# Expert stage of a two-block forward pass: split fp32r matmuls replaced by plain float32 on two column halves

## The chip, the cores and the metric

The kernel runs on one core of a Trainium2 chip. The metric is the device time of one execution in microseconds, the median of several runs. TensorE (PE in the profile), VectorE (DVE), ScalarE (ACT), GpSimd (POOL) and SyncE (SP) run side by side; SP issues the large transfers, and POOL issues the gathers and scatters that take their row numbers from a list.

## The reference, cut to what matters

Two blocks of layers run on 512 tokens of width 1024, all in float32. Only the last layer of the second block, a mixture of 32 experts, is touched here:

```python
expert = g_idx * EXP_PER_GROUP + e_idx           # 2 of 32 experts for each of 512 tokens
weights = g_p * e_p / jnp.sum(e_p, axis=-1, keepdims=True)
def block_mlp(args):                             # xb: the rows of one expert
    xb, e = args
    return (jax.nn.silu(xb @ w_gate[e]) * (xb @ w_up[e])) @ w_down[e]
y_pad = y_pad * w_pad[:, None]                   # each row by its token's weight
out = jax.ops.segment_sum(y_pad, tok_pad, num_segments=n_tok)
...
h = h + out                                      # then rmsnorm(h, final_norm_w) is the result
```

w_gate and w_up are 1024 x 512 and w_down is 512 x 1024 for each expert: 6 MiB an expert, 192 MiB (201.3 MB) in all.

## The kernel before

Everything but the expert layer is a chain of projections, scans and attention that fills the first 1,685 us. The weights of a product come in pieces of 1 MiB, [128, 4, 512] float32. ACT copies a piece to a rounded value (`w_hi`, type fp32r), DVE subtracts it from the raw piece (`w_lo`), and PE multiplies with both. In the trace an fp32r matmul is one matmul record, a plain float32 matmul is two, and a transpose is one.

The router gives each expert at most 64 rows (BLK = 64) with at most 15 overflow blocks after the 32 regular ones (none is needed for this input: 32 gathers run). DVE writes the token numbers of each expert's rows to `tok_of`, and POOL gathers those rows of the normalised input from `hn_dram` (`gather`, L855).

For each expert `e` the PE does, in this order (loop at the end of the tensor block):

- `gate_up(e)`: 32 fp32r matmuls of 512 columns (L1646, L1647). The stationary operand is `bT`, the 64 rows' high part beside their low part (128 columns), so one matmul gives both products; the moving operand is `e_hi` or `e_lo` (for the first two pieces `w_hi`, `w_lo`).
- `rows_T(e+1)`: 8 transposes that turn the next expert's rows (L1628).
- `down(e-1)`: 24 fp32r matmuls of 512 columns (L1667 to L1669), three for each product.
- `acts_T(e)`: 8 plain float32 matmuls with `fold`, which turn the activations and add the high and the low half (16 records at L1658; the timeline merges 8 for gate and 8 for up).

Beside that, for each expert, ACT makes six copies of a piece (L2286, L2303) and DVE six subtractions (L3164, L3280); ACT and DVE also split the rows and the activations. ACT copies the two halves of the result out (L2341), and POOL scatters them to `y_dram` by token number (L866). `y_dram` and `y_over` are zeroed earlier in the kernel (8 MiB, at 344 us). At the end SP reads `y_dram` back (`picked`, L688), DVE adds each token's two rows times their weights (`weighted`, L3330), and the last two experts' results (the `PAIR`) take another way: the last expert's `down` in plain float32 (`last_down`, L1687) and products with a matrix that puts rows to tokens (`pair_sums`, L1696), added by DVE at L3362.

Order is set by the instruction order in the source and by semaphores. SP fetches a piece of the next expert as soon as DVE has made its low part (`fetch`, L666), so one set of six raw pieces exists. In the first waits of the layer SP, POOL and the others meet at numbered stages (`together`).

## Time and profile before

| what | value |
|---|---|
| median of 3 runs | 2267.59 us (2263.74 to 2267.86) |
| profiled execution, first to last instruction (span) | 2262.9 us |
| median less span (what lies around the span, and the spread of runs) | 4.7 us |
| PE busy | 2186.2 us (97%) |
| DVE busy | 1478.4 us (65%) |
| ACT busy | 1248.5 us (55%) |
| mean granted TensorE clock | 0.987 |

The table of times holds no time of its own for the profiled execution beside its span. In the page, the busy digits are tenths in 40 slices of 56.6 us each. PE busy counts from a matmul's start to its modelled end, and matmuls overlap in the pipeline, so the pitch between starts tells the cost of one and not its duration. "128*64 128x512" means 128 contraction rows, 64 stationary columns, and a moving operand of 128 partitions x 512 columns.

### The profile page before, as it was taken

What the parts mean: (1) busy time and instruction counts of PE and PEld (TensorE: products, weight loads), DVE (VectorE), ACT (ScalarE), POOL (GpSimd) and SP (SyncE); (2) the same over time, 40 slices, a digit from 0 to 9 for tenths busy, and PEclk for the clock granted to TensorE, in tenths of its full rate; (3) what the DMA queues carried; (4) which work ended last, traced back from release to release, by engine and by line L of the source; (5) the groups of instructions that cost most, each with busy time, mean ns of one, the idle gap of its engine ahead of it and who ended that gap; (6) DMA issues with size and microseconds to landing.
All of it is one profiled execution on the core that took longest, in us unless ns stands there. A gap on an engine that the chain in (4) does not pass through costs nothing. (4 is left out here: it accounts for less than half of the span.)

```text
span 2262.9 us, 31931 instructions
## 1 busy us (share of the span) xinstructions
PE 2186.2 (97%) x12430; PEld 1731.7 (77%) x12430; DVE 1478.4 (65%) x1871; ACT 1248.5 (55%) x1696; POOL 303.7 (13%) x346
## 2 busy tenths in 40 slices
PE   7999999999999999999999999999995999999997
PEld 6878658877778787998888888888684777777774
DVE  3533862549988778765324573454447999988897
ACT  4324551468884455652315423244434889888885
POOL 2000001023320122640000000000011111122220
PEclk9999999999999999999999999999997999999999
DMA  7122117323224434011222213334146999999996
GB/s 241 57 74 93 38 38 249 124 90 93 93 84 158 148 115 150 3 59 56 90 97 93 93 43 126 112 113 149 56 155 248 399 405 412 403 404 398 401 401 255
DMA packets 121732, 385.61 MB, mean 170 GB/s; under 512 B 9549, under 2 KB 38533, under 8 KB 96401
## 3 DMA queue, kind: packets, MB, share of 16 engines
q1 hardware_dynamic: 106688, 333.54, 39.9%
q0 software_dynamic: 14416, 44.12, 5.7%
q10 hardware_dynamic: 512, 6.34, 0.7%
q8 instruction: 81, 1.33, 0.2%
q14 instruction: 35, 0.28, 0.0%
HBM read 362.89 MB, written 28.89 MB: 173 GB/s over the span
## 5 line engine op out<-in xcount | busy, mean ns | idle before, releaser
L2414 DVE TENSOR_TENSOR w_lo<-raw,w_hi 128x2048 fp32r<-128x2048 f32 x117 | 268.7, 2296 | 444.7 <-ACT w_hi L1757 444.5
L1757 ACT ACTIVATE w_hi<-raw 128x2048 fp32r<-128x2048 f32 x117 | 223.9, 1914 | 394.5 <-PE bank L918 358.2
L918 PE MATMUL bank<-hT_hi,w_hi 128*128 128x512 f32 x512 | 200.2, 391 | 2.5 <-DVE y_lo L3033 2.3
L918 PE MATMUL bank<-hT_lo,w_hi 128*128 128x512 f32 x512 | 199.5, 390 | 0.0
L918 PE MATMUL bank<-hT_hi,w_lo 128*128 128x512 f32 x512 | 199.4, 390 | 0.0
L1129 PE MATMUL bank<-hT_hi,w_hi 128*128 128x512 f32 x432 | 173.9, 402 | 0.9 <-DVE hT_lo L2478 0.9
L1129 PE MATMUL bank<-hT_hi,w_lo 128*128 128x512 f32 x432 | 168.2, 389 | 0.0
L1129 PE MATMUL bank<-hT_lo,w_hi 128*128 128x512 f32 x432 | 168.1, 389 | 0.0
L3280 DVE TENSOR_TENSOR e_lo<-eraw,e_hi 128x2048 fp32r<-128x2048 f32 x62 | 141.8, 2289 | 36.5 <-ACT e_hi L2303 35.3
L3164 DVE TENSOR_TENSOR e_lo<-raw,e_hi 128x2048 fp32r<-128x2048 f32 x64 | 146.6, 2290 | 8.2 <-ACT e_hi L2286 7.7
L3164 DVE TENSOR_TENSOR w_lo<-raw,w_hi 128x2048 fp32r<-128x2048 f32 x64 | 144.2, 2286 | 5.5 <-ACT w_hi L2286 5.4
L2286 ACT ACTIVATE e_hi<-raw 128x2048 fp32r<-128x2048 f32 x64 | 122.6, 1916 | 19.6 <-DMA raw<-expert_w_up 17.4
L2303 ACT ACTIVATE e_hi<-eraw 128x2048 fp32r<-128x2048 f32 x62 | 118.6, 1915 | 23.4 <-DMA eraw<-expert_w_down 21.6
L2286 ACT ACTIVATE w_hi<-raw 128x2048 fp32r<-128x2048 f32 x64 | 122.4, 1915 | 6.3 <-PE bank L1647 4.7
L918 PE MATMUL bank<-w_hi,hT_hi 128*128 128x512 f32 x288 | 112.4, 390 | 2.3 <-DVE fgate L2559 0.8
L918 PEld LDWEIGHTS bank<-hT_hi,w_hi 128*128 128x128 f32 x512 | 96.3, 188 | 23.1 <-DVE y_lo L3033 2.7
L918 PE MATMUL bank<-w_hi,hT_lo 128*128 128x512 f32 x288 | 112.1, 389 | 0.0
L918 PE MATMUL bank<-w_lo,hT_hi 128*128 128x512 f32 x288 | 112.1, 389 | 0.0
L918 PEld LDWEIGHTS bank<-hT_lo,w_hi 128*128 128x128 f32 x512 | 96.2, 188 | 20.1
L918 PEld LDWEIGHTS bank<-hT_hi,w_lo 128*128 128x128 f32 x512 | 96.3, 188 | 20.0
L1646 PE MATMUL bank<-w_hi,bT 128*128 128x512 f32 x256 | 104.2, 407 | 3.8 <-DVE bT L3291 2.9
L1667 PE MATMUL bank<-e_hi,aT_hi 128*64 128x512 f32 x248 | 99.1, 400 | 3.7 <-DVE aT_lo L3296 3.1
(609 smaller groups left out, 5194.1 us busy)
## 6 DMA issues: line engine op xcount, KB each, us to landing
raw<-expert_w_gate SPq DMA_DIRECT2D x64, 1024.0 KB
raw<-expert_w_up SPq DMA_DIRECT2D x64, 1024.0 KB
eraw<-expert_w_down SPq DMA_DIRECT2D x62, 1024.0 KB
raw<-w_in SPq DMA_DIRECT2D x40, 1024.0 KB
raw<-even_w_in SPq DMA_DIRECT2D x18, 1024.0 KB
raw<-odd_w_in SPq DMA_DIRECT2D x16, 1024.0 KB
raw<-even_w_out SPq DMA_DIRECT2D x8, 1024.0 KB
raw<-odd_w_out SPq DMA_DIRECT2D x8, 1024.0 KB
```

The lines of the kernel that those rows point to most:

```text
L918: mm = pe.matmul(out, st, mv, start=first and x == 0, stop=last and x == 2)
L1129: mm = pe.matmul(tall_bank(p, j)[:], st, mv, start=k == 0 and x == 0, stop=k == KD - 1 and x == 2)
L1646: pe.matmul(psum[u // 2][:], rows, e_hi[u][:, k], start=f == 0, stop=False)
L1667: pe.matmul(out, aT_hi[:, k], hi[:, w], start=k == 0, stop=False)
L1757: act.activation(split_to(m)[0][:], raw[n % RAW][:], ACT.Copy).then_inc(sem("hi_done"), 1)
L2286: act.activation(e_hi[u][:], eraw[u][:], ACT.Copy).then_inc(sem("gu_hi"), 1)
L2303: act.activation(e_hi[4 + u][:], eraw[4 + u][:], ACT.Copy).then_inc(sem("d_hi"), 1)
L2414: dve.tensor_tensor(split_to(m)[1][:], raw[split_of[m] % RAW][:], f32(split_to(m)[0][:]), ALU.subtract).then_inc(sem("lo_done"), 1)
L3164: dve.tensor_tensor(e_lo[u][:], eraw[u][:], f32(e_hi[u][:]), ALU.subtract).then_inc(sem("gu_lo"), 1)
L3280: dve.tensor_tensor(e_lo[4 + u][:], eraw[4 + u][:], f32(e_hi[4 + u][:]), ALU.subtract).then_inc(sem("d_lo"), 1)
```

## The change

The experts' weights are used raw. `gate_up` is 16 plain float32 matmuls with 64 stationary columns: for each of 8 contraction steps one for gate, to partitions 0 to 63 of a bank (the left column half of the array), and one for up, to partitions 64 to 127 (the right half). `down` is 8 such matmuls, one half for each 512 output columns. `acts_T` is four plain transposes. No scatter is left: the result, times the row weight (`ey`), goes through 8 products with a 0/1 matrix (`e_sel`, built by DVE) in which rows 0 to 63 give one half of the width and rows 64 to 127 the other; DVE adds their 8 tiles to the running sum in SBUF. Since no split pieces are needed, their room holds raw ones: three experts' weights are in flight. `y_dram`, `y_over`, their zeroing and the special way of the last two experts go, and the expert loop is written out rather than looped.

```diff
+    SETS, PIECES = 3, 6
...
+                sp.dma_start(pieces[e % SETS][k][:], expert(e, k)).then_inc(after(f"e_in{e % SETS}{k}", 0)[0], 16)
...
         together(sp, 20)
+        fetch(0, (4, 5))
+        fetch(1, (4, 5))
+        for k in range(RAW):
+            sp.wait_ge(sem("lo_done"), units[len(units) - RAW + k]["split"] + 1)
+            fetch(0, (k,))
+        together(sp, 21)
+        fetch(2, (5,))
+        for m in (len(split_of) - 2, len(split_of) - 1):
+            name, n = unit_free[m]
+            sp.wait_ge(sem(name), n)
+            fetch(1, range(2 * (m % SPL), 2 * (m % SPL) + 2))
+        sp.wait_ge(*after("rt_pe", 1))
+        fetch(2, (2, 3))
+        sp.wait_ge(*after("rt_exp", 1))
+        fetch(2, (4,))
+        sp.wait_ge(sem("hn_saved"), 16 * 2)
+        sp.wait_ge(*after("hnT_pe", KD))
+        fetch(2, (0, 1))
+        for e in range(SETS, NE):
+            old = e - SETS
+            sp.wait_ge(sem("gu_used"), 2 * old + 1)
+            fetch(e, (0, 2))
+            sp.wait_ge(sem("gu_used"), 2 * old + 2)
+            fetch(e, (1, 3))
+            sp.wait_ge(sem("d_used"), 2 * old + 1)
+            fetch(e, (4,))
+            sp.wait_ge(sem("d_used"), 2 * old + 2)
+            fetch(e, (5,))
...
-        load(hn_dram[2 * SEQ:], xs[0:1, 0], "hn_saved")
+        load(hn_dram[0:SEQ].rearrange("(t p) d -> p t d", p=P), xs[:], "hn_saved")
+        load(hn_dram[SEQ:], xs[0:1, 0], "hn_saved")
...
-        together(pool, 23)
-        pool.wait_ge(sem("hn_saved"), 16 * 3)
-        pool.wait_ge(*after("y_zero", 16 * 4))
+        pool.wait_ge(sem("hn_saved"), 16 * 2)
         pool.wait_ge(sem("xg_clear"), 1)
+        pool.wait_ge(sem("tok_there"), 1)
...
+            for half in HALVES:
+                mm = pe.matmul(psum[3][half, 0:BLOCKS + 1], hot_r[:, n], hot_t[:, n], start=n == 0, stop=n == 2 * NT - 1)
...
+        pe.wait_ge(*after("rt_taken", 3))
+        for n in range(2 * NT):
+            for half in HALVES:
+                mm = pe.matmul(psum[5][half, 0:BLOCKS + 1], hot_r[:, n], hot_b[:, n], start=n == 0, stop=n == 2 * NT - 1)
+        mm.then_inc(sem("rt_pe"), 1)
...
+        def gate_up(w, x, arrived):
+            for f in range(KD):
+                if f % 4 == 0:
+                    arrived(f // 4)
+                    arrived(2 + f // 4)
+                for half, rows in enumerate(HALVES):
+                    mm = pe.matmul(psum[GU_BANK][rows], x[:, f], w[2 * half + f // 4][:, f % 4], start=f == 0, stop=f == KD - 1)
+                if f % 4 == 3:
+                    mm.then_inc(sem("gu_used"), 1)
+        def acts_T():
+            for k in range(FF // P):
+                tr = pe.transpose(psum[H_BANK][:, k * P:k * P + P], gu_rows[:, k], ident)
+        def down(w, arrived):
+            for k in range(FF // P):
+                if k % 2 == 0:
+                    arrived(4 + k // 2)
+                for half, rows in enumerate(HALVES):
+                    mm = pe.matmul(psum[Y_BANK][rows], act_h[:, k], w[4 + k // 2][:, 2 * (k % 2) + half], start=k == 0, stop=k == FF // P - 1)
+                if k % 2:
+                    mm.then_inc(sem("d_used"), 1)
+        def sums(b, t, banks, name):
+            for half, rows in enumerate(HALVES):
+                pe.matmul(psum[banks[half]][:], e_sel[b][rows, t * P:t * P + P], ey[b][rows], start=True, stop=True).then_inc(sem(name), 1)
+        def sum_rows(e, t):
+            banks = (4 + 2 * (t % 2), 5 + 2 * (t % 2))
+            if t == 0:
+                pe.wait_ge(sem("ey_there"), e + 1)
+                pe.wait_ge(sem("e_sel"), e + 1)
+            if 8 * e + 2 * t - 2 > 0:
+                pe.wait_ge(sem("y_added"), 8 * e + 2 * t - 2)
+            sums(e % 2, t, banks, "y_sum")
+        pe.wait_ge(sem("x_rows"), 16)
+        rows_T()
+        for e in range(NE):
+            pe.wait_ge(sem("x_out"), e + 1)
+            gate_up(pieces[e % SETS], xT[e % 2], lambda k: pe.wait_ge(*piece_in(e, k)))
+            if e:
+                sum_rows(e - 1, 0)
+                sum_rows(e - 1, 1)
+            if e + 1 < NE:
+                pe.wait_ge(sem("x_rows"), 16 * (e + 2))
+                rows_T()
+            pe.wait_ge(sem("gu_out"), e + 1)
+            acts_T()
+            if e:
+                sum_rows(e - 1, 2)
+                sum_rows(e - 1, 3)
+            pe.wait_ge(sem("e_prod"), e + 1)
+            down(pieces[e % SETS], lambda k: pe.wait_ge(*piece_in(e, k)))
...
+        pe.wait_ge(sem("ey_there"), NE)
+        pe.wait_ge(sem("e_sel"), NE)
+        for t in range(NT):
+            if t < 2:
+                pe.wait_ge(sem("y_added"), 8 * (NE - 1) + 2 * t - 2)
+            sums((NE - 1) % 2, t, last_bank[t], "last_sum")
...
+        act.activation(mark_a[0:1, 2:3], mark_a[0:1, 1:2], ACT.Silu)
+        def x_out(x):
+            act.activation(x[:], psum[X_BANK][:].rearrange("p (k r) -> p k r", r=BLK), ACT.Copy).then_inc(sem("x_out"), 1)
+        def gu_out():
+            act.activation(gu_rows[:], psum[GU_BANK][:].rearrange("r (p k) -> r k p", k=FF // P), ACT.Copy).then_inc(sem("gu_out"), 1)
+        def silu_of_gate():
+            act.activation(silu_g[:], psum[H_BANK][:].rearrange("p (k r) -> p k r", r=P)[:, :, 0:BLK], ACT.Silu).then_inc(sem("e_silu"), 1)
+        act.wait_ge(sem("x_T"), 1)
+        x_out(xT[0])
+        for e in range(NE):
+            act.wait_ge(sem("gu_used"), 2 * e + 2)
+            gu_out()
+            if e + 1 < NE:
+                act.wait_ge(sem("x_T"), e + 2)
+                x_out(xT[(e + 1) % 2])
+            act.wait_ge(sem("h_T"), e + 1)
+            silu_of_gate()
+            act.wait_ge(sem("d_used"), 2 * e + 2)
+            act.activation(ey[e % 2][:], psum[Y_BANK][:], ACT.Copy, scale=rows_of[:, 1, e:e + 1]).then_inc(sem("ey_there"), 1)
...
+        dve.tensor_tensor(hot_t[:], hot_b[:], slot_id[:].unsqueeze(2).to_broadcast(wide), ALU.mult).then_inc(sem("rt_taken"), 1)
+        dve.tensor_tensor(hot_b[:], hot_b[:], weight[:].rearrange("p a t -> p (a t)").unsqueeze(2).to_broadcast(wide),
+                          ALU.mult).then_inc(sem("rt_taken"), 1)
+        dve.wait_ge(*after("rt_pe", 3))
+        dve.tensor_scalar(tok_of[:], psum[3][0:BLK, 0:BLOCKS + 1], float(NOBODY), row_end[0:BLK], ALU.add, ALU.min).then_inc(sem("tok_there"), 1)
...
+        def product():
+            dve.tensor_tensor(act_h[:], psum[H_BANK][:].rearrange("p (k r) -> p k r", r=P)[:, :, BLK:], silu_g[:], ALU.mult).then_inc(sem("e_prod"), 1)
+        def add_rows(t, half, bank, name):
+            r = resid[:, t, 512 * half:512 * half + 512]
+            dve.tensor_tensor(r, psum[bank][:], r, ALU.add).then_inc(sem(name), 1)
+        def added_rows(e, ts):
+            for t in ts:
+                for half in range(2):
+                    dve.wait_ge(sem("y_sum"), 8 * e + 2 * t + half + 1)
+                    add_rows(t, half, 4 + 2 * (t % 2) + half, "y_added")
+        def select(b, ids):
+            dve.tensor_scalar(e_sel[b][:], iota_tok, ids, None, ALU.is_equal).then_inc(sem("e_sel"), 1)
+        for e in range(NE):
+            if e:
+                added_rows(e - 1, (0, 1))
+            dve.wait_ge(sem("e_silu"), e + 1)
+            product()
+            if e:
+                added_rows(e - 1, (2, 3))
+            select(e % 2, rows_of[:, 0, e:e + 1])
```

On PE, in the loop over experts, these rows stand where `gate_up` of one expert ends (the last fp32r product of a low part, L1647), and the next rows' turning and the previous expert's `down` follow:

```order
L1647 MATMUL bank<-e_lo_267,bT 128x512
L1628 MATMUL bank<-masks,xg 128x64 x8
L1676 ISA
L1663 REGISTER_ALU
L1667 MATMUL bank<-e_hi_268,aT_hi 64x512
L1668 MATMUL bank<-e_lo_269,aT_hi 64x512
L1669 MATMUL bank<-e_hi_268,aT_lo 64x512
```

At the same place the changed kernel has (L1614 is `gate_up`, L1635 the 0/1 products of the expert before, L1604 the turning of rows, L1620 of activations, L1628 now `down`):

```order
L1614 MATMUL bank<-piece_276,xT_280 64x512
L1635 MATMUL bank<-ey_286,e_sel_288 128x512 x4
L1604 MATMUL bank<-masks,xg 128x64 x8
L1620 MATMUL bank<-masks,gu_rows 128x128 x4
L1635 MATMUL bank<-ey_286,e_sel_288 128x512 x4
L1628 MATMUL bank<-piece_277,act_h 64x512 x4
L1628 MATMUL bank<-piece_278,act_h 64x512 x4
L1614 MATMUL bank<-raw_51,xT_281 64x512
L1614 MATMUL bank<-raw_49,xT_281 64x512
```

`down` has moved from the next expert's turn into its own, behind the activations; the 0/1 products of the expert before stand in the two gaps in which `down` waits for ACT and DVE.

On SP, the fetches of the first experts' pieces (each 1 MiB) stand so before, the last of the straight code and with the semaphores that they wait for (`gu_lo` and `d_lo` count DVE's subtractions):

```order
L666 DMA eraw_262<-expert_w_down 128x2048 [waits d_lo]
L666 DMA eraw_263<-expert_w_down 128x2048 [waits d_lo]
L666 DMA raw_51<-expert_w_gate 128x2048 [waits gu_lo]
L666 DMA raw_52<-expert_w_gate 128x2048 [waits gu_lo]
L666 DMA raw_49<-expert_w_up 128x2048 [waits gu_lo]
L666 DMA raw_50<-expert_w_up 128x2048 [waits gu_lo]
```

and so in the changed kernel, at the end of the third expert's set and the start of the fourth's (`gu_used` and `d_used` count PE's groups; `g_kvT` stands for the turned rows of the router):

```order
L651 DMA piece_273<-expert_w_gate 128x2048 [waits g_kvT,hn_saved]
L651 DMA piece_274<-expert_w_gate 128x2048
L651 DMA raw_51<-expert_w_gate 128x2048 [waits gu_used]
L651 DMA raw_49<-expert_w_up 128x2048
L651 DMA raw_52<-expert_w_gate 128x2048 [waits gu_used]
L651 DMA raw_50<-expert_w_up 128x2048
L651 DMA piece_265<-expert_w_down 128x2048 [waits d_used]
L651 DMA piece_266<-expert_w_down 128x2048 [waits d_used]
```

A fetch now waits for the products of the expert three before, where it waited for DVE's subtractions from the expert one before.

## Rows read from the trace of the kernel before

**Rows 1.** Stretches of the expert loop: length, busy (x instructions), PEclk, DMA share, GB/s

```profile
1900.00:2000.00 100.00, 100.00 (x503) 75.85 (x503) 90.14 (x55) 88.65 (x81) 17.59 (x13) 1.00 1.02 406
2100.00:2200.00 100.00, 97.34 (x486) 72.83 (x486) 89.59 (x55) 85.70 (x79) 21.98 (x13) 1.00 1.01 400
```

**Rows 2.** Timeline of PE in the loop: start, length, engine, line, operation, out<-in, records

```profile
1747.29 1.17 PE L1628 MATMUL bank<-masks,xg 64*128 64x64 f32 x8
...
1953.37 1.17 PE L1628 MATMUL bank<-masks,xg 64*128 64x64 f32 x8
1954.47 0.45 PE L1667 MATMUL bank<-e_hi,aT_hi 128*64 128x512 f32 x1
...
1960.06 1.00 PE L1658 MATMUL bank<-fold,g_rows 128*128 128x64 f32 x8
...
1961.76 0.48 PE L1646 MATMUL bank<-w_hi,bT 128*128 128x512 f32 x1
...
1969.22 1.17 PE L1628 MATMUL bank<-masks,xg 64*128 64x64 f32 x8
...
2214.15 1.17 PE L1628 MATMUL bank<-masks,xg 64*128 64x64 f32 x8
```

**Rows 3.** What ACT waited for, 1750 to 2230 us: total, times, longest

```profile
ACT e_hi L2303 <- DMA eraw<-expert_w_down: 21.6, 25, 1.8
ACT e_hi L2286 <- DMA raw<-expert_w_up: 17.4, 19, 1.4
```

**Rows 4.** Timeline of PE where plain float32 products of half width or depth run

```profile
1297.57 3.71 PE L1440 MATMUL bank<-masks,forget 128*128 128x128 f32 x32 [0.69 <-ACT hv L1782]
...
1310.87 2.06 PE L1461 MATMUL bank<-hv,hkd 64*128 64x128 f32 x32
1312.85 1.97 PE L1478 MATMUL bank<-hstate,hqT 128*64 128x128 f32 x32
1314.75 1.96 PE L1487 MATMUL bank<-hv,hwithin 64*64 64x128 f32 x32
...
2237.94 7.08 PE L1687 MATMUL bank<-raw,act_h 128*64 128x512 f32 x16
2244.95 7.13 PE L1696 MATMUL bank<-masks,small 128*128 128x512 f32 x16
```

**Rows 5.** Groups by line, 1750 to 2263 us: busy, mean ns of one | idle before

```profile
L1668 PEld LDWEIGHTS bank<-e_lo,aT_hi 128*64 128x64 f32 x245 | 32.9, 134 | 20.7
L3286 DVE TENSOR_TENSOR act_h<-bank,silu_g 128x256 f32<-128x256 f32 x31 | 12.9, 417 | 5.4 <-ACT silu_g L2323 5.4
L2323 ACT ACTIVATE silu_g<-bank 128x256 f32<-128x256 f32 x31 | 11.6, 376 | 11.2 <-PE bank L1658 11.1
L2316 ACT ACTIVATE u_rows<-bank 128x512 f32<-128x512 f32 x30 | 17.5, 582 | 1.8 <-PE bank L1647 1.8
L3362 DVE TENSOR_TENSOR resid<-bank,resid 128x512 f32<-128x512 f32 x8 | 5.1, 683 | 0.3 <-DVE resid L3330 0.3
```

**Rows 6.** Timeline of DVE, POOL and PE at the start of the expert stage

```profile
1713.92 0.26 DVE L3274 TENSOR_SCALAR tok_of<-bank,row_end 64x48 int32<-64x48 f32 x1 [0.58 <-PE bank L1621]
...
1715.35 2.22 POOL L859 DMA_INDIRECT xg<-hn_dram,tok_of  x1 [26.46 <-issue]
...
1723.28 1.19 PE L1628 MATMUL bank<-masks,xg 64*128 64x64 f32 x8 [9.47 <-DMA xg<-hn_dram,tok_of]
1725.96 0.80 PE L1646 MATMUL bank<-w_hi,bT 128*128 128x512 f32 x1 [1.49 <-DVE bT L3291]
...
1730.40 0.42 PE L1646 MATMUL bank<-w_hi,bT 128*128 128x512 f32 x1
```

**Rows 7.** Timeline of DVE at the end of the kernel

```profile
2247.52 1.29 DVE L3362 TENSOR_TENSOR resid<-bank,resid 128x512 f32<-128x512 f32 x2 [0.32 <-DVE resid L3330]
...
2258.59 1.28 DVE L2461 SCALAR_TENSOR_TENSOR resid<-resid,small,last_gain 128x1024 f32<-128x1024 f32 x1
```

**Rows 8.** What PE waited for at L1628, whole kernel: total, times, longest

```profile
PE bank L1628 <- DMA xg<-hn_dram,tok_of: 9.5, 1, 9.5
```

461 lines of the change are left out of this document (92 added, 369 removed).

## Prediction

> **What bounds the kernel now.** I read the busy time by stretches first, then the timeline of PE inside the expert loop, then the waits. From 1750 to 2200 us PE is 97 to 100% busy at full clock, and the DMA engines are at a share of 1.01 with some 400 GB/s [rows 1]. DVE and ACT are at 90% of their time but not full. So two resources end together. One turn of the loop, from one turning of rows to the next, is 1969.22 - 1953.37 = 15.85 us, and in it PE matmuls follow each other without a gap [rows 2]. Over the 29 turns from 1747.29 to 2214.15 the mean is 466.86 / 29 = 16.10 us [rows 2]. The 0.25 us between is DMA: ACT waits 44 times for a piece, 39.0 us in all [rows 3], and since there is one set of raw pieces, what arrives late reaches PE through ACT and DVE. PE's loss, 29 x 0.25 = 7 us, is what is left of it. The stage is therefore PE's, with a transfer limit just behind.
>
> **What a plain float32 matmul costs.** Eight of them with 512 columns take 2244.95 - 2237.94 = 7.01 us for 16 records [rows 4]; about 0.15 of that is the change to another shape (below), so one costs 6.86 / 8 = 0.857 us. One fp32r matmul costs 0.23 us: between 1954.47 and 1960.06, 24 of them take 5.59 us [rows 2]. Per expert the change swaps 56 of 0.23 us for 32 of 0.857 us, which can only pay if two run at once.
>
> **Do two run at once?** The trace shows it at 128 columns. L1478 is the same form as the new `gate_up`: 64 stationary columns, the two matmuls of a pair to the two halves of one bank, different moving operands. Its 16 matmuls (32 records) take 1314.75 - 1312.85 = 1.90 us [rows 4]. In series they would take 16 x 0.857 / 4 = 3.43 us, side by side 8 x 0.214 = 1.71. So they overlap fully, with 0.19 over. L1461 is the form of the 0/1 products (64 contraction rows, two banks): 1.98 us for 16 [rows 4]. The 0.19 to 0.27 is partly the change of form at the group's start and partly per matmul; I take 0.15 for each change. At 512 columns nothing in this trace shows a pair. The bounds are 0.857 us a pair (full overlap) and 1.714 (none); I take 0.857, since the row nearest in form overlaps fully over a stretch of 1.9 us.
>
> The Trainium skill speaks against this: "TensorE: Matmul & The Clock Gate", Part 3, says that weight loads overlap running matmuls only where the row groups differ, and two column halves share theirs. By that rule the loads would stand in the open. The trace disagrees: a 64-column load is busy 134 ns [rows 5], and the 32 records at L1478 with a load each would need 4.3 us where 1.90 were taken. The skill's "TensorEngine Tiling (Array Packing)", Tiling Modes, says that a change of tiling mode drains TensorE; with the rows' 0.15 us for each change the trace agrees, and the sum holds four.
>
> **PE per expert after.**
> gate_up 8 pairs x 0.857 = 6.86; 0/1 products 4 pairs x 0.857 = 3.43; down 4 pairs = 3.43; rows_T as before, 1954.47 - 1953.37 = 1.10 [rows 2]; four transposes of 128 x 128 at (1301.2 - 1297.57) / 32 = 0.114, the length 3.71 less its overlap [rows 4], 0.46; four changes of form 0.60. Sum 15.88. The same way of adding gives for the loop before 56 x 0.23 + 1.10 for rows_T + 1.70 for acts_T (1961.76 - 1960.06 [rows 2]) = 15.68 against the 15.85 read, so it is good to about 0.2. I take 15.95 us, bounds 15.7 and 16.4.
>
> **What hides the rest.** From a turn's start: gate_up ends at 6.86; 0/1 products of tiles 0 and 1 run 7.0 to 8.75; rows_T to 9.85; transposes to 10.45; tiles 2 and 3 run 10.6 to 12.3; down from 12.45. ACT's copy of the gate_up bank (0.58 [rows 5]) is done near 7.7, needed at 10.0. DVE adds tile 0 from 8.05 and tile 1 until 10.7 (four of 0.68 [rows 5]); tile 3 needs tile 1's bank free at 11.45: slack 0.75. Silu 0.38 and product 0.42 [rows 5] behind the transposes end near 11.6; down needs them at 12.45: slack 0.85. The other four adds and the 0/1 matrix end near 15, needed in the next turn at 7. DVE falls from 90% to about 6.5 of 16 us, ACT to about 2.2; six copies and six subtractions an expert cost nothing before as long as PE hid them, and removing them gains only the 7 us of lateness they passed on.
>
> **DMA after.** The bytes of weights stay. A fetch now waits for the products of three experts back, so 29 experts' bytes have 31 turns to arrive. Even at the mean pace read before, 16.10 us an expert with a scatter beside it, 29 x 16.1 = 467 us are less than 31 x 15.95 = 494: transfers go off the path. A gather must land in about 14.5 us from the turning of the rows before; PE never waited for one in the loop before, where the same time was available [rows 8], where the one wait is the first.
>
> **The start.** tok_of ends at 1714.2, the gather is issued at 1715.35 behind a meeting of engines [rows 6]; now it waits for tok_of alone: -0.9 us. Of the time from the turning to the first gate_up (1723.28 to 1725.96 [rows 6]) the low part of the rows goes: -0.8. A second 0/1 set for the weights stands behind the first and is hidden by the gather's 8 us. So gate_up(0) starts at 1724.2. Its first 4.44 us ran at the clock's lower level after PE's idle 9.5 us (10 matmuls from 1725.96 to 1730.40, 0.444 us each [rows 6], against 0.23): 2.1 us lost, and again after. Expert 0 has no 0/1 products to fill its gaps: 6.86 + 2.1 + 0.15 + 1.10 + 0.46, then silu, product and handovers 1.3, down 3.43 = 15.4. It ends at 1739.6; 31 turns less the last rows_T are 31 x 15.95 - 1.1 = 493.35: the last down ends at 2233.0.
>
> **The end.** The copy with weight (0.58), the first two 0/1 products with their latency (1.2) and handovers put DVE's first last add at 2235.0. Before it stood at 2247.52 [rows 7], held up by eight weighted adds, `last_down` (7.01 us) and the read-back of y_dram, all of which go. From that add to the end the work is DVE's and ACT's and the same: unchanged 15.4 us. So the end moves by 2235.0 - 2247.52 = -12.5 us: span 2262.9 - 12.5 = 2250.4. The median shown lies 4.7 us above the profiled span, and I leave that as it is: 2267.59 - 12.5 = 2255. The zeroing at 344 us and half of the hn_dram save go too; PE has no wait there, so nothing for them.
>
> **Rivals.**
> (a) The gain is eaten by small extras: 0.15 to 0.55 us more a turn (per-matmul cost of a half, of two semaphores, a fifth drain). 31 x 0.25 to 31 x 0.5 gives 2263 to 2270. For it: L1461's 0.27 over, 0.12 more than I book. Against: the check above was off by 0.17 in all, and 0.07 of it is booked.
> (b) Slower: the fixed order of PE catches on DVE. Tile 3 of the 0/1 products stands in PE's queue before down and the whole next gate_up, and waits for DVE's adds of tile 1; down waits for the product queued behind those adds on DVE. The slacks are 0.75 and 0.85. Each us beyond costs 31 us; against the 12.5 gained it decides from 0.4 us a turn, that is from a lateness of 1.15 us of the adds. At 1 us a turn 2286. For it: four adds in one row on one engine; against: all lengths are read from this trace.
> (c) The halves do not overlap at 512 columns: 16 pairs x 0.857 x 31 = +425 us, 2680. Against it the 32 records of L1478. If only the loads of the 12 column pairs stood open, 12 x 4 x 0.134 x 31 = +199, 2454, which is the skill's rule above.
> (d) PE's changes of form are cheaper than booked and the DMA idle shows the turn at 15.6: 31 x 0.35 = 11 us less, 2244.
>
> **Chances.** The sum 0.58, in its own range 2248 to 2262; (a) 0.15, of which a small part stays faster; (b) with other new PE waits (a late gather, the written-out code's instruction fetches) 0.16; (c) 0.03; (d) 0.08. A change under 0.2% (4.5 us) can't be told from none here. Faster: 0.58 + 0.08 + 0.02 of (a) = 0.68; same: 0.13; slower: 0.19. The range goes from (d) at 2244 to the lighter part of (b), 2280, and leaves out (c) and what (b) holds above.
>
> **What would show it.** Turn of the loop by the start of rows_T: 15.95 us, the same early and late in the stage (before it grew with DMA). gate_up 16 matmuls in about 6.9 us with starts in pairs. No PE wait for DVE or for pieces in the loop; SP waits on PE, DMA share under 1.0 for parts of the stage. First last add near 2235. Wrong if PE waits appear before the 0/1 products of tile 3 or before down, if the turn is over 16.35 us, or if gate_up takes 13.7 us.

## The result, and the profile of the changed kernel

| | before | changed |
|---|---|---|
| median (lowest to highest) | 2265.66 us (2262.37 to 2267.86) | 2242.18 us (2241.57 to 2245.48) |
| span of the profiled execution | 2262.9 us | 2239.8 us |
| DVE, ACT busy | 65%, 55% | 53%, 39% |
| mean granted clock | 0.987 | 0.989 |

The ratio is 0.990, with a 95% interval of 0.9886 to 0.9914. The gain is 23.5 us, or 23.1 us between the two spans. The forecast was a gain of 12.5 us: right in direction and too small. The measured 2242.18 us lies 1.8 us below the lower end of the range, 2244 us. What a profile is read for below is one execution of each kernel; run 9 shows how far another execution of the changed kernel differs.

Stretches of the expert loop in the changed kernel (length, busy and instructions of PE, PEld, DVE, ACT, POOL, then PEclk, DMA share, GB/s):

```profile
1900.00:2000.00 100.00, 100.00 (x488) 40.29 (x486) 39.66 (x69) 14.51 (x26) 6.62 (x7) 1.00 1.01 406
2100.00:2200.00 100.00, 100.00 (x482) 39.45 (x479) 35.35 (x62) 14.13 (x25) 5.67 (x6) 1.00 0.88 349
```

Against [rows 1] DVE has fallen from 90% to 40%, PE is still full, and the share of the DMA engines falls below 1.00 in the last stretch, where the last fetches end. One turn of the loop on the timeline of PE (L1614 `gate_up`, L1635 0/1 products, L1604 and L1620 the turnings, L1628 `down`), an early one and the last start of `gate_up`:

```profile
1749.95 7.04 PE L1614 MATMUL bank<-piece,xT 128*64 128x512 f32 x32
1756.92 1.99 PE L1635 MATMUL bank<-ey,e_sel 64*128 64x512 f32 x8
1758.74 1.05 PE L1604 MATMUL bank<-masks,xg 64*128 64x64 f32 x8
1759.72 0.66 PE L1620 MATMUL bank<-masks,gu_rows 128*128 128x128 f32 x4
1760.31 1.99 PE L1635 MATMUL bank<-ey,e_sel 64*128 64x512 f32 x8
1762.22 3.65 PE L1628 MATMUL bank<-piece,act_h 128*64 128x512 f32 x16
1765.71 1.88 PE L1614 MATMUL bank<-raw,xT 128*64 128x512 f32 x7
...
2191.23 7.04 PE L1614 MATMUL bank<-raw,xT 128*64 128x512 f32 x32
...
2206.99 7.04 PE L1614 MATMUL bank<-piece,xT 128*64 128x512 f32 x32
```

From start to start a turn is 1765.71 - 1749.95 = 15.76 us early and 2206.99 - 2191.23 = 15.76 late. Before, PE's own turn was 15.85 and the mean 16.10 [rows 2]. PE's work an expert is thus nearly what it was: the gain does not come from cheaper products.

The start of the stage, DVE, POOL and PE, the rows that answer to [rows 6]:

```profile
1711.90 0.26 DVE L3153 TENSOR_SCALAR tok_of<-bank,row_end 64x48 int32<-64x48 f32 x1 [1.59 <-PE bank L1593]
1713.13 1.02 POOL L842 DMA_INDIRECT xg<-hn_dram,tok_of  x1 [24.63 <-DVE tok_of L3153]
1716.81 1.22 PE L1604 MATMUL bank<-masks,xg 64*128 64x64 f32 x8 [3.26 <-DMA xg<-hn_dram,tok_of]
1718.72 9.30 PE L1614 MATMUL bank<-raw,xT 128*64 128x512 f32 x32 [0.69 <-ACT xT L2249]
```

The first last add on DVE, answering to [rows 7]:

```profile
2224.38 1.29 DVE L3172 TENSOR_TENSOR resid<-bank,resid 128x512 f32<-128x512 f32 x2 [3.67 <-PE bank L1635]
```

The 23.1 us of span divide at two marks. The first gate_up starts at 1718.72 and not 1725.96: 7.2 us. From there to the first last add it takes 505.7 us and not 2247.52 - 1725.96 = 521.6: 15.9 us. The tail behind that add is 15.4 us in both.

The two marks are read in one execution of each kernel. What lies ahead of the stage, and is the same work in both, moves between executions too (run 9), so the first of the two parts is less firm than the second.

### The profile page after: what moved, and what is told of

It is laid out like the page before. It is cut to its first block, busy times and chain, and to the rows that moved or that the text cites. A ratio compares the mean times of both kernels' runs of the same rounds, so it can differ in the third digit from the quotient of the medians.

```text
span 2239.8 us, 29659 instructions
## 1 busy us (share of the span) xinstructions
PE 2171.6 (97%) x12338; PEld 1543.8 (69%) x12338; DVE 1179.4 (53%) x1888; ACT 871.1 (39%) x1411; POOL 231.8 (10%) x311
## 4 chain that ended last, share of the span: by engine, by line
PE 90%; DVE 7%; ACT 2%; issue 1%; DMA 1%; POOL 0%; SPq 0%; ACTq 0%; DVEq 0%; POOLq 0%
PE bank L889 38%; PE bank L1100 12%; PE bank L1614 10%; PE bank L1635 5%; PE bank L1628 5%; PE bank L1217 2%; PE bank L1113 2%; PE bank L1144 2%; PE bank L1604 1%; PE bank L1209 1%; PE bank L1046 1%; PE bank L1037 1%; PE bank L1620 1%; DVE w_lo L2304 1%; PE bank L1006 1%
## 5 line engine op out<-in xcount | busy, mean ns | idle before, releaser
L2304 DVE TENSOR_TENSOR w_lo<-raw,w_hi 128x2048 fp32r<-128x2048 f32 x117 | 268.6, 2296 | 446.0 <-ACT w_hi L1712 445.8
L1712 ACT ACTIVATE w_hi<-raw 128x2048 fp32r<-128x2048 f32 x117 | 223.9, 1913 | 395.6 <-PE bank L889 359.4
L3172 DVE TENSOR_TENSOR resid<-bank,resid 128x512 f32<-128x512 f32 x256 | 159.0, 683 | 306.0 <-PE bank L1635 306.0
L1614 PE MATMUL bank<-piece,xT 128*64 128x512 f32 x672 | 147.8, 592 | 0.0
L1635 PE MATMUL bank<-ey,e_sel 64*128 64x512 f32 x512 | 127.2, 615 | 0.8 <-ACT ey L2268 0.8
L1628 PE MATMUL bank<-piece,act_h 128*64 128x512 f32 x512 | 116.9, 598 | 1.0 <-DVE act_h L3167 1.0
L1614 PEld LDWEIGHTS bank<-piece,xT 128*64 128x64 f32 x672 | 48.3, 137 | 95.9 <-issue 95.9
L889 PEld LDWEIGHTS bank<-hT_hi,w_hi 128*128 128x128 f32 x512 | 96.6, 189 | 23.4 <-DVE y_lo L2922 2.7
L889 PEld LDWEIGHTS bank<-hT_hi,w_lo 128*128 128x128 f32 x512 | 96.7, 189 | 19.9
L2252 ACT ACTIVATE gu_rows<-bank 128x512 f32<-128x512 f32 x32 | 19.1, 598 | 200.9 <-PE bank L1614 200.9
L1100 PEld LDWEIGHTS bank<-hT_hi,w_hi 128*128 128x128 f32 x432 | 81.1, 188 | 22.3 <-issue 5.9
L1100 PEld LDWEIGHTS bank<-hT_hi,w_lo 128*128 128x128 f32 x432 | 81.1, 188 | 19.3 <-issue 3.1
```

What stands on the lines that cost most here:

```text
L889: mm = pe.matmul(out, st, mv, start=first and x == 0, stop=last and x == 2)
L1100: mm = pe.matmul(tall_bank(p, j)[:], st, mv, start=k == 0 and x == 0, stop=k == KD - 1 and x == 2)
L1614: mm = pe.matmul(psum[GU_BANK][rows], x[:, f], w[2 * half + f // 4][:, f % 4], start=f == 0, stop=f == KD - 1)
L1628: mm = pe.matmul(psum[Y_BANK][rows], act_h[:, k], w[4 + k // 2][:, 2 * (k % 2) + half], start=k == 0, stop=k == FF // P - 1)
L1635: pe.matmul(psum[banks[half]][:], e_sel[b][rows, t * P:t * P + P], ey[b][rows], start=True, stop=True).then_inc(sem(name), 1)
L1712: act.activation(split_to(m)[0][:], raw[n % RAW][:], ACT.Copy).then_inc(sem("hi_done"), 1)
```

## The experiments

Spans are compared with spans of one profiled execution. The profiled execution's time is 1.8 to 2.2 us above its span in these runs.

**1. Do the column halves pay?** Both matmuls of a pair go to one half (the results are others):

```diff
-                    mm = pe.matmul(psum[GU_BANK][rows], x[:, f], w[2 * half + f // 4][:, f % 4], start=f == 0, stop=f == KD - 1)
+                    mm = pe.matmul(psum[GU_BANK][LOW], x[:, f], w[2 * half + f // 4][:, f % 4], start=f + half == 0, stop=f + half == KD)
...
-                    mm = pe.matmul(psum[Y_BANK][rows], act_h[:, k], w[4 + k // 2][:, 2 * (k % 2) + half], start=k == 0, stop=k == FF // P - 1)
+                    mm = pe.matmul(psum[Y_BANK][LOW], act_h[:, k], w[4 + k // 2][:, 2 * (k % 2) + half], start=k + half == 0, stop=k + half == FF // P)
```

> The changed kernel with one edit: both matmuls of a pair in gate_up and in down go to the same column half of the bank (they add up there, so the experts' results are not those of the reference). The matmuls, loads, columns and bytes are the same in number. Theory: what pays for plain float32 is that the two column halves run side by side, a pair of 512 columns in one 0.857 us. Then these 12 pairs an expert take 24 x 0.857 instead of 12 x 0.857 us, gate_up 13.7 instead of 6.97 us, the turn 15.76 + 10.3 = 26.0 us, and the span about 2239.8 + 32 x 10.3 = 2569 us. Rival: the matmuls of a pair follow each other anyway and each is simply cheaper than 0.857 us, with 64 stationary columns 0.43: then the turn stays at 15.8 us and the span within 2 us of 2240.

Measured: span 2573.0 us. The timeline of PE, one turn:

```profile
1774.40 13.90 PE L1614 MATMUL bank<-piece,xT 128*64 128x512 f32 x32
1788.23 1.99 PE L1635 MATMUL bank<-ey,e_sel 64*128 64x512 f32 x8
...
1793.54 7.08 PE L1628 MATMUL bank<-piece,act_h 128*64 128x512 f32 x16
1800.46 4.88 PE L1614 MATMUL bank<-raw,xT 128*64 128x512 f32 x11
```

The same 32 records take 13.83 us and not 6.97, the turn 26.06. A pair at 512 columns overlaps fully, and the overlap is worth 333 us. One matmul here takes 13.83 / 16 = 0.864 us with its loads included, against the 0.857 us read for one before, so even with both in one half no load shows. The rival (no overlap, each matmul cheaper) falls.

**2 and 3. Why was the first gather so much faster?** In the kernel before, first SP's fetches alone are held back until the gather's rows are there, then DVE's subtractions (on which those fetches wait):

```diff
-        fetch(1, 1, GU)
+        fetch(1, 1, GU[:3])
+        sp.wait_ge(sem("x_rows"), 16)
+        fetch(1, 1, GU[3:])
```

```diff
+        dve.wait_ge(sem("x_rows"), 16)
         gu_lo(0, (3,))
         d_lo(0, range(2))
```

> The kernel before, with SP's fetches from the second expert's last up piece on held back until the first gather's rows have landed (before, they are issued at 1717.03 and 1718.91 us, between the gather's issue at 1715.35 and its rows at 1723.28). Theory A: the gather was late because the weights' packets stood in the DMA engines ahead of it: from tok_of's end to the turning of rows 9.1 us fall to 5.5 to 6.5, with POOL's own 2.2 us unchanged. Theory B (POOL makes the gather's descriptors slowly while DVE runs its 128x2048 subtractions): no change here, 9.1 us.

> The kernel before, with DVE's first three 128x2048 subtractions behind tok_of held back until the first gather's rows have landed; the fetches that wait for them are thereby later too. Both theories: POOL's instruction for the gather falls from 2.2 to about 1.0 us if DVE's work slowed it (B), and stays 2.2 if not. By A alone the time from tok_of's end to the turning of rows is the same as in the run with later fetches; by B it is 1.2 us less than there; if both hold it comes near the 4.65 us of the changed kernel plus the 0.9 us of the meeting of engines, 5.5 us.

Measured with later fetches (span 2258.0), on POOL, DVE and PE:

```profile
1711.53 0.26 DVE L3276 TENSOR_SCALAR tok_of<-bank,row_end 64x48 int32<-64x48 f32 x1 [0.58 <-PE bank L1623]
1712.00 2.29 DVE L3166 TENSOR_TENSOR e_lo<-raw,e_hi 128x2048 fp32r<-128x2048 f32 x1
1712.95 2.22 POOL L861 DMA_INDIRECT xg<-hn_dram,tok_of  x1 [26.24 <-issue]
1717.99 1.19 PE L1630 MATMUL bank<-masks,xg 64*128 64x64 f32 x8 [6.57 <-DMA xg<-hn_dram,tok_of]
```

With the gather alone (span 2261.8):

```profile
1711.84 0.26 DVE L3274 TENSOR_SCALAR tok_of<-bank,row_end 64x48 int32<-64x48 f32 x1 [0.58 <-PE bank L1621]
1713.26 1.02 POOL L859 DMA_INDIRECT xg<-hn_dram,tok_of  x1 [26.21 <-issue]
1716.97 1.19 PE L1628 MATMUL bank<-masks,xg 64*128 64x64 f32 x8 [5.24 <-DMA xg<-hn_dram,tok_of]
```

From tok_of's start to the turning of the rows it was 1723.28 - 1713.92 = 9.36 us before [rows 6]. Without the weights' fetches it is 6.46 (2.90 less), without DVE's work as well 5.13 (1.33 less), and in the changed kernel 4.91. Both causes hold. What is left, 0.22 us, is the meeting of engines that the forecast had priced at 0.9: from tok_of's start to the start of POOL's instruction it is 1.42 to 1.43 us in the kernel before and in these two, and 1.23 in the changed one.

The spans say less. With later fetches the span is 4.9 us shorter, but 2.4 us of that lie ahead of the edit: tok_of starts at 1711.53 and not 1713.92. With the held subtractions gate_up(0) starts only at 1724.38, behind three of them, so that what the gather gains is lost again.

**4. DVE's work alone beside the gather**, in the changed kernel: two subtractions of 128x2048 that nothing reads, right behind tok_of, and no transfer added:

```diff
+        for _ in range(2):
+            own(dve.tensor_tensor(junk_a[:], resid_2, resid_2, ALU.subtract))
+            own.wait()
```

> The changed kernel with two 128x2048 subtractions on DVE, which nothing reads, right behind tok_of, beside the first gather; no DMA is added. Theory: POOL's instruction takes 2.2 us and not 1.02, and the rows are turned 1.2 us later, 6.1 us after tok_of's start and not 4.9. Rival: POOL's 2.2 us came from SP's fetches, and both stay as they are.

Measured (span 2244.6), DVE, POOL and PE:

```profile
1715.71 0.26 DVE L3155 TENSOR_SCALAR tok_of<-bank,row_end 64x48 int32<-64x48 f32 x1 [1.58 <-PE bank L1595]
1715.89 4.60 DVE L3157 TENSOR_TENSOR junk_a<-resid 128x2048 fp32r<-128x2048 f32 x2
1716.95 2.12 POOL L844 DMA_INDIRECT xg<-hn_dram,tok_of  x1 [25.89 <-DVE tok_of L3155]
1721.85 1.22 PE L1606 MATMUL bank<-masks,xg 64*128 64x64 f32 x8 [4.48 <-DMA xg<-hn_dram,tok_of]
```

6.14 us from tok_of's start to the turning, as expected. There is more in it: the gather's instruction ends at 1719.07, which is 0.9 us behind the end of the subtraction that ran when it began (1715.89 + 2.29 = 1718.18). With later fetches it is the same: 1712.00 + 2.29 = 1714.29, and 1715.17. In both POOL had begun some 1 us into the subtraction, so they can't tell a stop from a mere slowing. The loop of the kernel before can, since there the gathers begin at other points of a subtraction. DVE and POOL, twice:

```profile
1765.06 2.28 DVE L3164 TENSOR_TENSOR e_lo<-raw,e_hi 128x2048 fp32r<-128x2048 f32 x1
1765.08 3.08 POOL L859 DMA_INDIRECT xg<-hn_dram,tok_of  x1 [8.09 <-PE bank L1628]
...
1780.92 2.29 DVE L3164 TENSOR_TENSOR e_lo<-raw,e_hi 128x2048 fp32r<-128x2048 f32 x1
1781.73 2.27 POOL L859 DMA_INDIRECT xg<-hn_dram,tok_of  x1 [8.58 <-issue]
```

The gather that begins 0.02 us into the subtraction takes 3.08 us, the one that begins 0.81 us into it takes 2.27, and both end 0.8 us behind the subtraction's end (1768.16 against 1767.34, 1784.00 against 1783.21). One that begins 1.51 into it, at 1955.31, takes 1.60. In the changed kernel, which has no such subtraction in the stage, all 32 gathers take 0.94 to 1.02 us. So POOL stands still until the subtraction that it meets has ended, and then does its work. The next instruction of DVE is not held up by it: it starts at 1783.12, before the gather's instruction ends, and takes its usual 0.68 us. A gather that begins together with a subtraction, at 1796.77, takes 0.93 us: only a subtraction already under way holds it.

The Trainium skill, "SBUF — State Buffer", section "SBUF: two separate sides", says that the pair of ports that DVE and GpSimd share is an exclusive lock, held for a whole instruction, and that a DVE operation with two SBUF inputs takes it only against a GpSimd operation that reads SBUF. The trace agrees as far as it goes: the subtraction has two SBUF inputs, the gather's instruction reads tok_of, and it waits the whole subtraction out. That the ports are what it waits for no run here shows.

**5. What kept the loop before at 16.10 us?** In the kernel before half of each down piece is left out of the loop's fetches (the results are others):

```diff
+        def fetch_half(e, k):
+            sp.wait_ge(sem("d_lo"), 2 * e + (k - 5))
+            sp.dma_start(eraw[k][:, 0:2], expert(e, k)[:, 0:2]).then_inc(sem(f"e_in{k}"), 16)
...
-            fetch(e, e, DN)
+            for k in DN:
+                fetch_half(e, k)
```

> The kernel before, in which from the third expert on only half of each down piece is fetched (the other half keeps what the piece held; 5 MiB an expert instead of 6, so the results of down are others). All instructions of PE, DVE and ACT are the same. Theory: the 0.25 us a turn above PE's own 15.85 us, 7 us in all, is the DMA engines' lateness, which three sets in flight took away in the changed kernel: then the turn is 15.85 us from early to late and the span 6 to 8 us below that of the kernel before. Rival: the 7 us come from DVE and ACT, which are at 90%, and their handovers: then the turn stays at 16.1 us and the span within 1.5 us.

Measured: 2256.29 us against 2263.91, ratio 0.9966 (0.9953 to 0.9978), span 2253.4. The turnings on PE's timeline, and a stretch:

```profile
1745.62 1.17 PE L1633 MATMUL bank<-masks,xg 64*128 64x64 f32 x8
...
2189.52 1.17 PE L1633 MATMUL bank<-masks,xg 64*128 64x64 f32 x8
```

```profile
2000.00:2100.00 100.00, 100.00 (x504) 74.82 (x504) 92.56 (x58) 89.66 (x83) 13.98 (x13) 1.00 0.95 346
```

(2189.52 - 1745.62) / 28 = 15.85 us, flat, with ACT and DVE as full as before. The medians differ by 7.6 us. The 29 x 0.25 = 7 us of lateness were the DMA engines' alone. The rival falls.

**6 and 7. Are three sets what took it away?** In the changed kernel a fetch waits for the expert two before, or for the one just before:

```diff
-            old = e - SETS
+            old = e - 2          # seventh run: e - 1
```

> The changed kernel, in which a fetch waits for the products of the expert two before, not three (the three sets loaded ahead of the loop stay). Theory: the DMA engines need 6.29 MB / 405 GB/s = 15.5 us an expert and PE 15.76, so with a whole expert's time in hand two sets do as well: PE does not wait, and the span is within 1 us. Rival: the third set is needed, since the engines must stay full over the uneven order of gate, up and down pieces: PE waits for pieces in each turn, 0.2 to 0.5 us, and the span is 6 to 15 us longer.

> The changed kernel, in which a fetch waits for the products of the expert just before. Now about 12 us lie between the end of one use of a piece and its next, and six pieces take 15.5 us to fetch. Theory: PE waits for DMA in each turn, turn 16.5 to 20 us, span 20 to 120 us longer; this is the price of in-flight sets that the kernel before avoided by copying pieces to their split form. Rival: under 5 us longer.

Measured: with two sets 2244.17 us (2241.43 to 2246.31), ratio to the kernel before 0.9905 (0.9887 to 0.9923), and no PE wait for a piece between 1750 and 2200. With one set the span is 2247.2. PE's waits there, and the second and the last start of `gate_up`:

```profile
PE bank L1614 <- DMA raw<-expert_w_up: 2.5, 3, 1.7
PE bank L1614 <- DMA piece<-expert_w_up: 2.5, 4, 1.0
```

```profile
1733.13 7.04 PE L1614 MATMUL bank<-piece,xT 128*64 128x512 f32 x32
...
2214.42 7.04 PE L1614 MATMUL bank<-piece,xT 128*64 128x512 f32 x32
```

Two sets do as well as three: from the first gate_up to the first last add it takes 505.7 us with both. (The span with two sets, 2243.8 us, is longer only ahead of that: gate_up(0) starts at 1722.68, as late as in run 9.) One set does not. Thirty turns take 2214.42 - 1733.13 = 481.29 us and not 2206.99 - 1734.19 = 472.80: 8.5 us of lateness, of which the waits listed show 5.0; beyond them single gate_ups take up to 7.38 us where 7.04 is usual. That is about what the kernel before lost, 7 us. My expectation for one set, 20 to 120 us, was wrong by far, and so was the rival's under 5. I had added the use of a set and its fetch in series, but pieces are released one by one, and while one is in use the five others travel.

So the second set is what takes the lateness away in the changed kernel, and the third adds nothing. Whether one set here is late for the same reason as the one set of raw pieces before, which had ACT's and DVE's step between landing and use and a scatter beside it, is not shown.

**8. The clock at the start.** Ten plain float32 matmuls that nothing reads fill PE's idle gaps in the router:

```diff
+        idle_work(4)
         pe.wait_ge(*after("rt_taken", 1))
...
+        idle_work(4)
         pe.wait_ge(*after("rt_taken", 2))
...
+        idle_work(2)
         pe.wait_ge(sem("x_rows"), 16)
```

> The changed kernel with ten plain float32 matmuls of 512 columns that nothing reads in PE's idle gaps of the router: four before each of the two long waits for DVE (6.8 us each) and two before the wait for the first gather. Theory: the granted clock is 0.5 from the router's products to the middle of the first gate_up because PE had idled; with this work it is 1.0 there, gate_up(0) takes 7.0 us instead of 9.3, and the span is 2 to 4 us shorter. Rival: the gaps are too short or the work too little to bring the clock back, and at the low level the extra matmuls (1.71 us each there) make the router's products late: span 0 to 3 us longer.

Measured: 2242.28 us (2238.43 to 2244.27), ratio to the kernel before 0.9903 (0.9886 to 0.9919), span 2236.6. PE:

```profile
1715.90 1.17 PE L1611 MATMUL bank<-masks,xg 64*128 64x64 f32 x8 [0.19 <-DMA xg<-hn_dram,tok_of]
1717.75 7.09 PE L1621 MATMUL bank<-raw,xT 128*64 128x512 f32 x32 [0.69 <-ACT xT L2257]
```

Here gate_up(0) takes 7.09 us and not 9.30. From tok_of's start (1710.79) to the turning of the rows it takes 5.11 us and not 4.91, so the added work made the rows 0.2 us late. The price of the lower level, 2.1 us in the forecast, is real. The granted clock was 0.50 from the router's products on; with the added matmuls it was back at 1.00 before gate_up(0). Run 12, with the same work in it, has 7.09 us too, but in run 11 it left gate_up(0) at 8.78 us. In the medians 2.2 us can't be told from the spread of the executions, and of the 3.2 us by which this span is shorter 1.2 lie ahead of the added work (the router's first product starts at 1685.37 and not 1686.56). So the mechanism is shown in two executions of three, and it is not a gain that can be relied on.

**9 and 10. The changed kernel again, and with the zeroing of 8 MiB at 344 us kept.**

```diff
+        for y in (y_dram, y_over):
+            for half in range(2):
+                load(y[SEQ * half:SEQ * half + SEQ].rearrange("(p r) (k n) -> p (r k) n", p=P, n=D // 4),
+                     zeros[:].unsqueeze(1).to_broadcast([P, 4 * NT, D // 4]), "y_zero")
```

> The changed kernel, not edited, beside the three others of this group. Its time should be 2242 us within 1.5, as in the first measurement; the executions lie in two groups some 4 us apart (2241.6 to 2242.7 and 2245.5 so far), as those of the kernel before do (2262.4 to 2264 and 2267 to 2268).

> The changed kernel with the zeroing of the 8 MiB of y_dram and y_over at 344 us put back, though nothing uses them. Theory: no engine waits for DMA there, so the span is the same within 0.5 us, and none of the gain came from its removal. Rival: the 8 MiB at some 400 GB/s, 21 us of DMA time, hold weights back there, 1 to 5 us longer.

Measured: 2245.59 us (2244.0 to 2245.99) and 2245.95 us (2242.69 to 2246.44), each with a ratio of 0.9913 to the kernel before (0.9899 to 0.9926, and 0.9900 to 0.9927). The zeroing has no cost that shows. The changed kernel itself came out 3.4 us above its first median, outside what I expected (2242 within 1.5), so between groups of runs 2 to 4 us are open. Against its own kernel before it gains 19.1 us here and 23.5 in the first comparison.

The two profiled executions of the changed kernel show where they part. The router's products on PE, in the first comparison and in run 9:

```profile
1686.56 8.44 PE L1585 MATMUL bank<-w_router,hnT 128*128 128x36 f32 x64
```

```profile
1688.91 9.58 PE L1585 MATMUL bank<-w_router,hnT 128*128 128x36 f32 x64
```

The products start 2.35 us later and take 1.14 us longer, in the same kernel and ahead of the changed stage. gate_up(0) starts at 1722.21 and not 1718.72, only 3.8 us earlier than before, and from there to the first last add it takes 506.2 us (505.7 in the first). From tok_of's start to the turning of the rows it takes 4.91 us in both. So the second part of the gain, 15.4 to 15.9 us, and the faster gather belong to the change; up to 3.5 us at the start belong to the execution. The kernel before moves in the same way: its products start at 1686.18, and in its variants of runs 2, 3, 5 and 13 at 1684.0 to 1684.6.

**11. A faster kernel: 0/1 products in fp32r.** ACT writes the weighted result rounded, DVE makes the low part, and 16 fp32r matmuls stand where 8 plain ones were. First alone, then with the idle work of run 8:

```diff
+            for y in (ey, ey_lo):
+                for half, rows in enumerate(HALVES):
+                    mm = pe.matmul(psum[banks[half]][:], e_sel[b][rows, t * P:t * P + P], y[b][rows], start=y is ey, stop=y is ey_lo)
...
+            dve.scalar_tensor_tensor(ey_lo[b][:], psum[Y_BANK][:], w, f32(ey[b][:]), ALU.mult, ALU.subtract).then_inc(sem("ey_lo"), 1)
```

> The changed kernel with its 0/1 products in fp32r: ACT writes the weighted result rounded (ey), DVE makes its low part (one scalar_tensor_tensor of 128x512 more an expert), and 16 fp32r matmuls in row-half pairs take the place of 8 plain float32. Theory: a pair of fp32r matmuls of 512 columns takes 0.23 us, so the products take 8 x 0.23 = 1.84 us an expert and not 3.73, PE's turn falls to 13.9 us, PE runs ahead until the DMA engines, which are full in the changed kernel until 2188 us, set the end: the last piece lands near 2188, the first last add comes near 2193 to 2197 instead of 2224.4, and the span is 2208 to 2215 us, 25 to 31 us below the changed kernel. Rival: two fp32r matmuls in the row halves do not run side by side: 16 x 0.23 = 3.7 us, turn 15.7 us, span 2237 to 2240. Rival: DVE's extra instruction makes PE wait at down or at tile 3 of the products: turn above 14.5 us already in the first ten experts.

> The changed kernel with both edits: 0/1 products in fp32r and PE's idle gaps in the router filled with ten matmuls. Theory: the idle work makes gate_up(0) 2.2 us shorter, so the refetching of expert 0's pieces starts 2.2 us earlier, and since the DMA engines then bound the loop, the end moves by the same: 2.2 us below the kernel with fp32r products alone (2217.9), 2215.7, about 48 us below the kernel before. Rival: the end is set by pieces whose order does not change, the gain is under 0.5 us.

Measured: 2217.91 us, ratio 0.9788 (0.9770 to 0.9805), span 2218.4; with idle work 2215.51 us, ratio 0.9782 (0.9769 to 0.9796), span 2213.2. Against the changed kernel, by the ratios to the kernel before, they gain 25 us (0.990 to 0.9788) and 30 us (0.9913 to 0.9782, side by side). PE's timeline of the second, an early turn and a late one, then its waits from 1750 to 2190 us:

```profile
1732.50 7.04 PE L1622 MATMUL bank<-piece,xT 128*64 128x512 f32 x32
1739.47 0.50 PE L1644 MATMUL bank<-ey,e_sel 64*128 64x512 f32 x2
...
1740.50 1.05 PE L1612 MATMUL bank<-masks,xg 64*128 64x64 f32 x8
...
1746.91 7.04 PE L1622 MATMUL bank<-piece,xT 128*64 128x512 f32 x32
...
2132.75 3.60 PE L1622 MATMUL bank<-piece,xT 128*64 128x512 f32 x16
2137.86 3.65 PE L1622 MATMUL bank<-piece,xT 128*64 128x512 f32 x16 [1.50 <-DMA piece<-expert_w_up]
```

```profile
PE bank L1622 <- DMA piece<-expert_w_up: 8.7, 7, 1.8
PE bank L1622 <- DMA raw<-expert_w_up: 4.6, 4, 1.5
```

The row halves run side by side in fp32r too: tiles 0 and 1 take 1740.50 - 1739.47 = 1.03 us for 8 matmuls, where in series they would take 1.84. The turn is 14.41 us and not the 13.9 expected (tiles 2 and 3 take more), and late in the loop PE waits for pieces, as expected. The span of the first, 2218.4, is above the 2208 to 2215 expected; its gate_up(0) starts at 1723.05, 4.3 us later than in the changed kernel's first profile.

The gain of the second over the first can't be told by the medians. That its median is the 2215.5 expected is luck: the added work shortened gate_up(0) by 0.4 us only (9.22 to 8.78), not by 2.2. By the profiles gate_up(0) starts 5.5 us earlier (1717.55 against 1723.05) and the span is 5.2 us shorter, so the end does move with the start. But those 5.5 us lie ahead of the added work: the router's products start 3.7 us earlier (1685.39 against 1689.13) and take 1.75 us less (8.35 against 10.10).

**12. Is that kernel bound by transfers?** Half of each down piece is left out of the loop's fetches (the results are others):

```diff
-            fetch(e, (4,))
...
-            fetch(e, (5,))
+            for k in (4, 5):
+                sp.wait_ge(sem("d_used"), 2 * old + k - 3)
+                sp.dma_start(pieces[e % SETS][k][:, 0:2], expert(e, k)[:, 0:2]).then_inc(after(f"e_in{e % SETS}{k}", 0)[0], 16)
```

> The kernel with both edits, with only half of each down piece fetched from the fourth expert on (the rest of a piece keeps what it held, so the results are others). Theory: in the kernel with fp32r products the 12 us that PE waits for pieces late in the loop are the DMA bound; with 5 MiB an expert PE never waits, every turn is 14.42 us and the span is 10 to 14 us below that with all bytes. Rival: the waits come from the order or release of pieces and stay: under 3 us.

Measured: span 2197.3, 15.9 us less, a little more than expected; gate_up(1) starts at the same time in both (1732.44 and 1732.50). No PE wait for a piece is left. From 1732.44 to 2164.93 PE makes 30 turns of 14.42 us. So late pieces cost the kernel with both edits some 16 us.

**13 and 14. The clock in the router.** Does the work of ACT and DVE beside PE make the granted clock fall earlier? ACT's copies and DVE's subtractions moved away in the kernel before; put beside in the changed one (ACT's part of each edit is shown):

```diff
-        gu_hi(0, range(3), True)
         act.wait_ge(*after("rt_exp", 1))
...
         act.wait_ge(*after("rt_pe", 1))
+        gu_hi(0, range(3), True)
```

```diff
+        for n in range(3):
+            act.activation(junk_a[:], resid_2, ACT.Copy).then_inc(sem("junk"), 1)
```

> The kernel before, with ACT's three 128x2048 copies and DVE's three subtractions that run beside the router's products (1687 to 1696 us) moved behind them. Theory (the work of the other engines beside PE makes the clock fall earlier): the 64 products take 8.4 to 10.1 us, as in the changed kernel, not 10.6 to 10.85. Rival (it comes from something else, the phase at which PE's work falls): 10.6 us or more. The span says little here, since the moved work is later in the way of the first expert: 0 to 8 us longer.

> The changed kernel with three 128x2048 copies on ACT and three 128x2048 subtractions on DVE, which nothing reads, beside the router's products. Theory: the 64 products take 10.6 us or more, gate_up(0) starts about 2 us later than without at the same start of the products. Rival: 8.4 to 10.1 us as in the changed kernel so far.

Measured, the router's products in each (spans 2263.8 and 2243.8):

```profile
1684.38 11.02 PE L1614 MATMUL bank<-w_router,hnT 128*128 128x36 f32 x64
```

```profile
1688.89 9.66 PE L1587 MATMUL bank<-w_router,hnT 128*128 128x36 f32 x64
```

Neither follows the theory: without the copies 11.02 us, with them 9.66, where run 9 has 9.58 without them. The theory falls. What was to be explained is this, two stretches of PE alone (length, busy, PEclk, DMA share, GB/s), first of the kernel before, then of the changed one:

```profile
1688.00:1690.00 2.00, 2.00 (x18) 0.87 1.02 358
```

```profile
1692.00:1694.00 2.00, 2.00 (x14) 0.62 1.03 338
```

The stretches ahead of them are at 1.00 and those behind at 0.50. The clock so falls at 1688.00 + 2 x 0.37 / 0.50 = 1689.5 in the one, 3.3 us after the first of the 64 products (1686.18), and at 1692.5 in the other, 5.9 us after it (1686.56), with PE busy throughout. But it is no fixed difference of the two kernels. In run 9, the changed kernel again, the clock falls 4.7 us after the first product (1688.91; the granted clock is 0.90 from 1692 to 1694 us), and the 64 products take 9.58 us; in run 12, a variant of it, they take 10.29. The kernel before and its variants have 10.6 to 11.0. Why the fall comes when it does stays open.

## Why the prediction was wrong in size

Forecast 2255.0, measured 2242.2: 12.8 us. Two steps of the forecast failed: the sum of the turn, which was 5.9 us too large over the loop, and the start, where the gather's time was taken as fixed, 3.5 us. The rest of the miss is 2.0 us that the profiled execution happened to have ahead of the stage and 2.3 us in the step from span to median, less 0.8 of small terms. By its own steps:

- **Two halves side by side: right.** gate_up 16 matmuls in 6.97 us (6.86 + 0.15 said); run 1 shows the price without it. Rival (c) had nothing, with or without the loads.
- **The turn, 15.95 us: 0.19 too long, 31 x 0.19 = 5.9 us, the largest term.** In the rows above the turn is 6.97 + 1.82 + 0.98 + 0.59 + 1.91 + 3.49 = 15.76. The sum had taken rows_T with 1.10, read where it stood behind an fp32r product, so one change of form was in it already and was booked again; 0.98 in its place gives 15.88 - 0.12 = 15.76. Expert 0 of the changed kernel shows that: there rows_T stands right behind gate_up, another form, and takes 1729.05 - 1727.95 = 1.10 us; in the later turns it stands behind the 0/1 products, which have 64 contraction rows as it has, and takes 0.98.

```profile
1727.95 1.17 PE L1604 MATMUL bank<-masks,xg 64*128 64x64 f32 x8
1729.05 0.65 PE L1620 MATMUL bank<-masks,gu_rows 128*128 128x128 f32 x4
```

  The other 0.07 was a margin put on top. The bounds 15.7 to 16.4 held the turn.
- **The cover on DVE, ACT and DMA: right.** No wait of PE for DVE, ACT or a piece from 1750 to 2200; rival (b) had nothing. Of the three sets two are needed: with one set 8.5 us are lost, with two none (runs 6 and 7). That the lateness before was DMA's, 7 us, is shown by run 5.
- **The start: 5.5 us too late. The step that failed in its mechanism: 3.5 of them.** "A second 0/1 set for the weights stands behind the first and is hidden by the gather's 8 us", and "-0.9" for the meeting, took the gather's time as fixed. It was not a gather's time but a gather's under load: 2.90 us of it were weights' packets ahead of it, 1.33 were DVE's subtractions, and both go with the change. The meeting was worth 0.2. That is 4.45 us and not 0.9. The 0.8 for the low part of the rows was right (0.77).
- **The other 2.0 us of the start** are tok_of's earlier start, from the router's products, 8.44 us and not 10.85 at a clock that fell later. It was in no step. It is not the change's: in run 9 the same kernel has tok_of at 1715.39, later than before. The median of that group, 2245.6, would have lain inside the range, but its gain of 19.1 us is still well above the 12.5 said.
- **The price of the clock's lower level, 2.1 us: right** (run 8), and expert 0 took 15.47 us, 15.4 said. The forecast put the low level down to "PE's idle 9.5 us"; the granted clock had been 0.50 since the router's products, 1689.5 us, long before that idle time.
- **The end: right.** From the last down's end (2218.71 + 3.49 = 2222.20) to the first last add 2.2 us, 2.0 said; the tail 15.4. Of the 15.9 us between the two marks some 7 were lateness and 29 x 0.09 = 2.6 the turn. The 6 us left are put down to what the end gave up (`last_down`, the weighted adds and the read-back); no run measures them apart.
- **Span to median.** The 4.7 us put on top came from one execution against a median of others. In the first comparison it was 2.4, and a profiled execution's own time is about 2 us over its span: 2.3 us of the miss.
- **Zeroing: right**, nothing that shows (run 10).

5.5 + 5.1 (5.9 less 0.8 of small terms, most of them behind the last gate_up) + 2.3 = 12.9 us. Rival (d), a turn of 15.6 us and 2244, was nearest in number, and that by luck: the turn was 15.76, and the rest of its miss came from the start and from the 4.7 us.
